# Semaphores set by four engines, routing without its own norm stage, and a last norm in half rows: a two-part transformer stack on one core

## The reference

```python
def layer_norm(x, g, b):
    xf = x.astype(jnp.float32)
    mu = jnp.mean(xf, -1, keepdims=True)
    var = jnp.mean(jnp.square(xf - mu), -1, keepdims=True)
    return ((xf - mu) * lax.rsqrt(var + LN_EPS) * g + b).astype(x.dtype)

def moe_swiglu(h2, w_router, w_gate, w_up, w_down):
    logits = (h2 @ w_router).astype(jnp.float32)
    top_logits, top_idx = lax.top_k(logits, TOP_K)
    top_w = jax.nn.softmax(top_logits, axis=-1)
...
    hid = jax.nn.silu(lax.ragged_dot(xs, w_gate, sizes)) * lax.ragged_dot(xs, w_up, sizes)
    y = lax.ragged_dot(hid, w_down, sizes)
...
        h = layer_norm((DN_ALPHA * h + mix).astype(h.dtype), ln_mix_g[layer], ln_mix_b[layer])
            ff = moe_swiglu(h.reshape(B * S, D), moe_router[j], moe_w_gate[j], moe_w_up[j], moe_w_down[j])
        h = layer_norm((DN_ALPHA * h + ff).astype(h.dtype), ln_ffn_g[layer], ln_ffn_b[layer])
```

## Time and profile before

| what | us |
|---|---|
| median of 3 runs (lowest, highest) | 3354.91 (3353.01, 3355.23) |
| the profiled execution, its own time | 3353.27 |
| its span, first to last instruction | 3351.4 |
| PE busy | 3111.8 |
| DVE busy | 2402.8 |
| ACT busy | 1788.5 |
| POOL busy | 189.6 |
| mean granted TensorE clock, share of full speed | 0.962 |

### The profile page before, as it was taken

The page is one execution under the profiler, slowest core; times in us unless marked ns, Lnnn a source line. Parts: engine busy times, 40 slices in busy tenths (PEclk is TensorE's granted clock), DMA queues, the critical chain, the costliest instruction groups (busy, mean ns, idle before and its releaser), DMA issues. The chain is left out here.

```text
span 3351.4 us, 46020 instructions
## 1 busy us (share of the span) xinstructions
PE 3111.8 (93%) x18426; PEld 2722.4 (81%) x18426; DVE 2402.8 (72%) x2698; ACT 1788.5 (53%) x2115; POOL 189.6 (6%) x101
## 2 busy tenths in 40 slices
PE   6998899998899899989998999996999999999997
PEld 5887688876688798988888998886888888888885
DVE  4664566898766666555766666655999999889997
ACT  3444444433244455544444454443777777777775
POOL 0000000002400001110000021100000000000000
PEclk9998899999999899999999999997999999999998
DMA  4552255443155433343554433433999999999995
GB/s 164 190 192 100 84 188 208 165 162 125 63 188 188 177 141 120 137 142 133 181 189 159 143 126 126 152 128 152 364 354 355 355 355 354 355 356 355 353 358 201
DMA packets 97415, 698.65 MB, mean 208 GB/s; under 512 B 10960, under 2 KB 11472, under 8 KB 13776
## 3 DMA queue, kind: packets, MB, share of 16 engines
q1 hardware_dynamic: 97232, 696.11, 56.2%
HBM read 693.97 MB, written 1.05 MB: 207 GB/s over the span
## 5 line engine op out<-in xcount | busy, mean ns | idle before, releaser
L890 PE MATMUL ps<-weight_high,act_parts 128*128 128x512 f32 (+2 forms) x2656 | 749.8, 364 | 13.7 <-DVE act_parts L2698 3.8
L890 PEld LDWEIGHTS ps<-weight_high,act_parts 128*128 128x128 f32 x2656 | 480.8, 191 | 93.1 <-issue 10.2
L890 PE MATMUL ps<-weight_low,act_parts 128*128 128x512 f32 (+2 forms) x1456 | 516.4, 355 | 0.0
L861 PE MATMUL ps<-act_parts,weight_high 128*128 128x512 f32 x1760 | 459.6, 395 | 9.4 <-DVE weight_low L716 8.6
L861 PEld LDWEIGHTS ps<-act_parts,weight_high 128*128 128x128 f32 x1760 | 319.1, 190 | 70.3 <-DVE weight_low L716 11.0
L890 PE MATMUL ps<-act_parts,weight_low 128*128 128x256 f32 x1312 | 374.5, 285 | 0.0
L669 ACT ACTIVATE weight_high<-ring 128x2048 fp32r<-128x2048 f32 x108 | 206.7, 1915 | 311.3 <-PE ps L861 232.8
L890 PE MATMUL ps<-act_parts,weight_high 128*128 128x256 f32 x1792 | 335.9, 289 | 6.9 <-DVE weight_low L2554 5.7
L716 DVE TENSOR_TENSOR weight_low<-ring,weight_high 128x2048 fp32r<-128x2048 f32 x108 | 247.3, 2291 | 126.7 <-ACT weight_high L669 126.7
L2554 DVE TENSOR_TENSOR weight_low<-ring,weight_high 128x2048 fp32r<-128x2048 f32 x82 | 190.2, 2320 | 199.3 <-PE ps L890 131.9
L890 PEld LDWEIGHTS ps<-weight_low,act_parts 128*128 128x128 f32 x1456 | 280.2, 192 | 35.8 <-issue 1.0
(11 more groups left out here) (444 smaller groups left out, 5811.4 us busy)
## 6 DMA issues: line engine op xcount, KB each, us to landing
ring<-in_l_moe_up SPq DMA_DIRECT2D x110, 1024.0 KB, 4.9
ring_more<-in_l_moe_down SPq DMA_DIRECT2D x110, 1024.0 KB, 4.9
ring<-in_l_w_in SPq DMA_DIRECT2D x92, 1024.0 KB, 4.8
vtm<-in_l_moe_gate SPq DMA_DIRECT2D x55, 1024.0 KB, 4.9
merged<-in_l_moe_gate SPq DMA_DIRECT2D x55, 1024.0 KB, 4.9
ring<-in_l_ffn_down SPq DMA_DIRECT2D x52, 1024.0 KB, 4.8
ring<-in_l_ffn_up SPq DMA_DIRECT2D x35, 1024.0 KB, 4.8
ring_more<-in_l_ffn_gate SPq DMA_DIRECT2D x32, 1024.0 KB, 4.7
```

Of the source, the lines that this page charges most:

```text
L861: return c.nc.tensor.matmul(c.ps[:, bank, :], still, c.act[:, k, :, :].rearrange("p s t -> p (s t)"), start=k == 0, stop=k == KD - 1, skip ...
L890: ins = nc.tensor.matmul(out, still[a], moving[b], start=first and n == 0, stop=last and n == 2, skip_group_check=True)
```

## The change

1. The block that set the semaphores is gone. `start_stage` issues its loads on SyncE without waiting for it, and the other four engines each set a quarter of the semaphores (39) at the beginning of that stage.
2. `norm_stage` is gone; `route_stage` takes its work. x is turned after scaling by the statistics alone. ScalarE applies gain and offset per column while it evicts each of eight pairs of 128x128 blocks, and TensorE makes the logits of a pair as soon as it is evicted. Beside that VectorE applies the gain and offset rows to x, and ScalarE makes the high part of x.
3. The comparisons of both row tiles are made in one instruction each. The products that count each list come before those that place the rows.
4. The low part of x, the softmax weights, and the high and low parts of weight units 0 and 1 move behind the branch, into `experts_stage`; for the skipped dense way a block `weights_stage` repeats the weights.
5. SyncE loads the rows of the last norm at the end of `route_stage`. The last norm works on half rows with two fused instructions each and stores each half.
6. Each engine loads `most` once and keeps it in its register for the later guarded blocks.

```diff
-def when(c):
+def when(c, name):
 
     def wrap(body):
         if c.condition is None:
             return body
 
         def guarded(eng):
-            with eng.If(c.condition(eng.value_load(c.most, min_val=0, max_val=T))):
+            if name not in c.most_loaded:
+                c.most_loaded[name] = eng.value_load(c.most, min_val=0, max_val=T)
+            with eng.If(c.condition(c.most_loaded[name])):
                 body(eng)
         return guarded
...
-def norm_stage(c, gain, offset, units):
...
+        @block.sync
+        def _(sp):
+            for n, row in enumerate(rows):
+                sp.dma_start(c.rowbuf[:, n, :], row.partition_broadcast(P)).then_inc(gains.sem, 16)
+            for u in range(MOE_UNITS_AHEAD):
+                units.load(sp, u)
+            sp.wait_ge(scaled.sem, scaled.base + 4)
+            for n, row in enumerate(last_rows):
+                sp.dma_start(c.rowbuf[:, n, :], row.partition_broadcast(P)).then_inc(gains.sem, 16)
 
...
         @block.vector
         def _(dve):
             link = lambda ins: c.vchain(dve, ins)
             V = nc.vector
+            for t in range(TT):
+                for h in range(2):
+                    link(V.bn_stats(small[:, 32 + 16 * t + 6 * h:38 + 16 * t + 6 * h], x[:, t, 512 * h:512 * h + 512]))
+                link(V.bn_aggr(small[:, 16 + 2 * t:18 + 2 * t], small[:, 32 + 16 * t:44 + 16 * t]))
+                V.tensor_scalar(small[:, t:t + 1], small[:, 17 + 2 * t:18 + 2 * t], LN_EPS, None, ALU.add)\
+                    .then_inc(summed.sem, 1)
+            for t in range(TT):
+                dve.wait_ge(rooted.sem, rooted.base + t + 1)
+                link(V.reciprocal(small[:, 6 + t:7 + t], small[:, 2 + t:3 + t]))
+                V.tensor_scalar(x[:, t, :], x[:, t, :], small[:, 16 + 2 * t:17 + 2 * t], small[:, 6 + t:7 + t],
+                                ALU.subtract, ALU.mult).then_inc(normed.sem, 1)
+            dve.wait_ge(gains.sem, gains.base + 32)
+            for t in range(TT):
+                dve.wait_ge(packed.sem, packed.base + (1, 5)[t])
+                V.tensor_tensor(x[:, t, :], x[:, t, :], c.rowbuf[:, 0, :], ALU.mult).then_inc(scaled.sem, 1)
+                dve.wait_ge(scaled.sem, scaled.base + 2 * t + 1)
+                V.tensor_tensor(x[:, t, :], x[:, t, :], c.rowbuf[:, 1, :], ALU.add).then_inc(scaled.sem, 1)
             dve.wait_ge(logits_made.sem, logits_made.base + 1)
+            link(V.tensor_copy(logits, ps[:, 0:TT, 0:E]))
+            other = logits.unsqueeze(2).to_broadcast([P, TT, E, E])
+            own = logits.unsqueeze(3).to_broadcast([P, TT, E, E])
+            V.tensor_tensor(choice.above, other, own, ALU.is_gt)
+            link(V.tensor_tensor(choice.equal, other, own, ALU.is_equal))
+            link(V.tensor_tensor(choice.equal, choice.equal, lower.unsqueeze(1).to_broadcast([P, TT, E, E]), ALU.mult))
+            link(V.tensor_tensor(choice.above, choice.above, choice.equal, ALU.add))
+            link(V.tensor_reduce(choice.rank, choice.above, axis=AX.X, op=ALU.add))
+            V.tensor_scalar(one, choice.rank, 0.0, None, ALU.is_equal)
+            link(V.tensor_scalar(two, choice.rank, 1.0, None, ALU.is_equal))
+            V.tensor_tensor(r.chosen, one, two, ALU.add).then_inc(chosen_made.sem, 1)
+            link(V.tensor_tensor(choice.tmp, one, two, ALU.subtract))
+            link(V.tensor_tensor(choice.tmp, choice.tmp, logits, ALU.mult))
+            link(V.tensor_reduce(s(0), choice.tmp, axis=AX.X, op=ALU.add))
             V.tensor_scalar(s(1), s(0), -1.0, None, ALU.mult).then_inc(diff_made.sem, 1)
             dve.wait_ge(placed.sem, placed.base + 1)
+            link(V.tensor_reduce(s(5)[:, 0:1], ps[:, 3, 0:E], axis=AX.X, op=ALU.max))
+            link(V.tensor_copy(r.most, s(5)[0:1, 0:1]))
+            dve.wait_ge(placed.sem, placed.base + 2)
             link(V.tensor_copy(r.place, ps[:, 2, 0:2 * E].rearrange("p (t e) -> p t e", t=TT)))
 
...
         @block.scalar
         def _(act):
+            for t in range(TT):
+                act.wait_ge(summed.sem, summed.base + t + 1)
+                nc.scalar.activation(small[:, 2 + t:3 + t], small[:, t:t + 1], ACT.Sqrt).then_inc(rooted.sem, 1)
+            for n in range(KD):
+                k = n // 2 + 4 * (n % 2)
+                act.wait_ge(packed.sem, packed.base + 2 + k % 4)
+                nc.scalar.activation(c.hT[:, k, :], norm_bank(c, k), ACT.Identity, scale=gain[:, k:k + 1],
+                                     bias=offset[:, k:k + 1]).then_inc(unloaded.sem, 1)
+            for t in range(TT):
+                act.wait_ge(scaled.sem, scaled.base + 2 * t + 2)
+                nc.scalar.activation(c.x_parts[0][:, t, :], x[:, t, :], ACT.Copy).then_inc(x_parts.sem, 1)
             act.wait_ge(diff_made.sem, diff_made.base + 1)
             nc.scalar.activation(s(2), s(1), ACT.Exp).then_inc(exp_made.sem, 1)
+
+        @block.tensor
+        def _(pe):
+            for t in range(TT):
+                pe.wait_ge(normed.sem, normed.base + t + 1)
+                for b in range(4):
+                    for k in (b, b + 4):
+                        last = nc.tensor.transpose(norm_bank(c, k)[:, P * t:P * t + P], x[:, t, P * k:P * k + P], c.ident)
+                    if t == 1 or b == 3:
+                        last.then_inc(packed.sem, 1)
+            for n in range(KD):
+                k = n // 2 + 4 * (n % 2)
+                pe.wait_ge(unloaded.sem, unloaded.base + n + 1)
+                for t in range(TT):
+                    last = nc.tensor.matmul(ps[:, t, 0:E], c.hT[:, k, P * t:P * t + P], router[:, k, :], start=(n == 0),
+                                            stop=(n == KD - 1))
+            last.then_inc(logits_made.sem, 1)
+            pe.wait_ge(chosen_made.sem, chosen_made.base + 1)
+            for t in range(TT):
+                last = nc.tensor.matmul(ps[:, 3, 0:E], c.ones, r.chosen[:, t], start=(t == 0), stop=(t == TT - 1))
+            last.then_inc(placed.sem, 1)
+            nc.tensor.matmul(ps[:, 2, 0:E], earlier, r.chosen[:, 0], start=True, stop=True)
+            nc.tensor.matmul(ps[:, 2, E:2 * E], earlier, r.chosen[:, 1], start=True, stop=False)
+            nc.tensor.matmul(ps[:, 2, E:2 * E], c.ones, r.chosen[:, 0], start=False, stop=True).then_inc(placed.sem, 1)
...
+def weigh_choice(c, dve, r, choice):
+
+    V, s = c.nc.vector, choice.column
+    link = lambda ins: c.vchain(dve, ins)
+    link(V.tensor_scalar(s(3), s(2), 1.0, None, ALU.add))
+    link(V.reciprocal(s(4), s(3)))
+    link(V.tensor_tensor(s(5), s(2), s(4), ALU.mult))
+    for t in range(TT):
+        link(V.tensor_scalar(choice.tmp[:, t], choice.two[:, t], s(5)[:, t:t + 1], None, ALU.mult))
+        link(V.scalar_tensor_tensor(out=r.weight[:, t], in0=choice.one[:, t], scalar=s(4)[:, t:t + 1], in1=choice.tmp[:, t],
+                                    op0=ALU.mult, op1=ALU.add))
+
+
+def weights_stage(c, r, choice):
+
+    with c.nc.Block() as block:
+        @block.vector
+        @when(c, "vector")
+        def _(dve):
+            weigh_choice(c, dve, r, choice)
 
 
...
                 pe.wait_ge(picked.sem, picked.base + e + 1)
+                if part:
+                    pe.wait_ge(x_parts.sem, x_parts.base + 3)
...
+            units.make_high(act, 0)
             for half in range(2):
                 take_gathered(0, half, half)
+            units.make_high(act, 1)
...
             pick(0)
+            dve.wait_ge(x_parts.sem, x_parts.base + 2)
+            nc.vector.tensor_tensor(c.x_parts[1], c.x, c.x_parts[0].bitcast(F32), ALU.subtract).then_inc(x_parts.sem, 1)
+            weigh_choice(c, dve, r, choice)
+            units.make_low(dve, 0)
             for half in range(2):
                 take_gathered(0, half, 2 + half)
+            units.make_low(dve, 1)
...
-    norm_stage(c, gain, offset, units)
-    route_stage(c, router, lower, earlier, r, units)
+    choice = Choice(c)
+    route_stage(c, rows, columns, last_rows, router, lower, earlier, r, units, choice)
     chain = c.vchain
     c.condition, c.vchain = lambda most: most <= SLOTS, c.gathered_chain
-    experts_stage(c, r, iota, units, ALPHA)
+    experts_stage(c, r, iota, units, ALPHA, choice)
     c.condition, c.vchain = lambda most: most > SLOTS, c.dense_chain
+    weights_stage(c, r, choice)
     spread_stage(c, r.weight, c.cat)
     ffn_stage(c, *weights, G, EXPERTS, c.cat, keep=ALPHA, add=1.0, ahead=units.loaded)
     c.condition, c.vchain = None, chain
...
+    sems = [s.sem for s in c.sig.values()]
...
         @block.scalar
         def _(act):
+            for sem in sems[0::4]:
+                nc.scalar.sem_inc(sem, START)
...
-            for n, row in enumerate(rows):
-                sp.dma_start(c.rowbuf[:, n, :], row.partition_broadcast(P)).then_inc(gains.sem, 16)
             for t in range(TT):
-                sp.wait_ge(added.sem, added.base + t + 1)
-                sp.dma_start(out[:, t, :], x[:, t, :]).then_inc(stored.sem, 16)
```

(21 more changed lines are left out.)

193 lines of the change are left out of this document (59 added, 134 removed).

## The result

The changed kernel took 3328.11 us (median of 4 runs, 3327.14 to 3328.75), the kernel before 3353.96 us (4 runs, 3351.13 to 3355.23): a ratio of 0.9921, 95% interval 0.9910 to 0.9933. The forecast was 3327.4. The profiled execution took 3328.18, with a span of 3326.1 for 3351.4, so 25.3 us are to be found in the trace. Several of the kernels here now and then have a run some 6 to 10 us longer (five of the 34 runs of the kernel before that stood beside the experiments lay at 3360 to 3365 us), and in the two profiles that caught one, those of the experiments with 26 full products and with `most` loaded each time, the loss lies in the first 1000 us or so, far from the change.

A forecast was written before the change was run, and what follows sets the result against it. TensorE, busy 93%, was taken as the bound, so only its idle places counted: 12.8 (start) + 10.2 (ahead of experts) + 3.7 (end) = 26.7 off 3353.27 gives 3326.6; half of 1.64 added, 3327.4. Range 3322.0 to 3334.0.

The forecast's parts named there:

- the cover: Start: 39 increments per engine, at most 3.3 us, hidden by the 5.78 us from x's load issue to first work.
- the start does not shrink: Start: the 13 us are something other than increments, so only 13.9 us stays of the gain, 3340.2 us; chance 5%.
- The template of the mixer's norm: Ahead of the experts: mixer's norm timings reused after the statistics, first transpose +4.6 us, first eviction +7.0, transposes end +8.3.
- The lower clock level: Routing logits: 32 instructions at a 0.20 us cadence on TensorE, taking 6.4 us and ending at +14.7.
- the rival of 32%: Routing: logits run at the higher clock level, paced by evictions, 3.2 us less, 3324.2 us; chance 32%.
- The cover behind the branch: Picks to first product: work moved onto VectorE takes 8.3 us, just under the 8.58 us there; thin by 0.3.
- The SyncE queue's seventh load: Experts' start: loads 7 and 8 go some 7 us after the branch, wanted most of a 17.9 us step later; nothing waits.
- the rival of a lasting lag of VectorE: Experts' loop: VectorE enters later and stays late, 0.6 us TensorE wait per step, 33 us, so 3360; chance 2%.
- 0.3 + 3 x (0.3 + b): End: skipped-stage boundaries, b between 0 and 1.24, taken 0.4: 2.4 us for 3.39, gain 1.0.
- three now, without a load: End: three skipped stages that no longer load the count, part of the 1.0 us gain there.
- The half-row operation: Last norm: four half-row operations of 0.69 us each (bounds 0.64 and 0.75), norm 5.9 us for 6.98, gain 1.0.
- A dear branch: End: skipped stages costing 1.5 us more than now; with thin covers, 3329 to 3334 us, chance 9%.

The follow-up runs named there:

- the last kernel: Changed kernel with 18 full products ahead of the routing transposes and the 156 increments shared by three engines, none on TensorE: 3324.75 us, run again 3324.23 us.

## Why the prediction was right

The gains were forecast at 26.7 us off the profiled execution, and the trace has 25.3: 0.54 less at the start, 0.10 less ahead of the experts, 0.27 less at the end and 0.60 lost between, against 0.11 in the loop. That the median came within 0.7 us of 3327.4 is in part luck: the forecast had 0.82 added for the distance between median and profiled execution, and the changed kernel shows no such distance (3328.11 and 3328.18).

**The start**, forecast 12.8, measured 12.26. The issue at 0.75 was right (0.74), and so was the cause. The step that was off by half a microsecond is the cover: the increments were priced at 84 ns on every engine and put at 3.3 us. They are 73 ns on ScalarE, 93 on VectorE and about 80 on GpSimd, but 154 on TensorE, whose 39 held the barrier past the landing of the loads; without them the first work came at 6.80, 6.80 and 6.62 in three profiles instead of 7.08. The rival "the start does not shrink" rested on no row showing an increment; the packed trace of the kernel before had all 156 of them, up to 13.20 us. The rule of the Trainium skill, "Advanced Engine Details and Errata", DMA Bandwidth Details, that an increment costs about a cycle, does not hold for increments as instructions in a queue: by it the start would not have shrunk.

**Between the start and the routing** the forecast had nothing and 0.60 went. It is no term of the change: none of the experiments touches this part, and those without an early loss took between 2268.9 and 2271.2 us over it.

**Ahead of the experts**, 10.2 against 10.10. The template of the mixer's norm gave the transposes (+4.6, measured +4.58) and the evictions (+7.0, +7.01). The lower clock level was the right choice against the rival of 32%: the logits ran at 1.2 GHz throughout. They began at +8.05 for +8.3 and took 6.83 us, not 6.4, and VectorE's copy behind them began at +14.92 for +14.7; its chain to the choice took 2.2 for 2.3, and the picks came at +21.28 for +21.2. The rival was sound in what it would pay: at the higher level, held there by full products, the first product came 3.1 to 3.7 us earlier in four profiles, and the forecast had put 3.2 on it. The cover behind the branch held to its thin margin: 8.58 us from picks to product, the same as before, with 0.46 us of room on VectorE. The SyncE queue's seventh load went out at 2304.82 and nothing waited for it.

**The loop** did as the forecast said: 1004.38 for 1004.49 us, and the rival of a lasting lag of VectorE did not come. The number is not that firm in itself: over all profiles this stretch takes either 1002.7 to 1002.8 or 1004.1 to 1004.7 us, and the two profiled runs of the last kernel have one each, 1002.7 and 1004.6 (from their first product, 2302.19 and 2301.77, to their statistics of the last norm, less the skipped stages).

**The end**, forecast 3.7, measured 3.43, by errors that nearly cancel. The early rows gave 1.56 for 1.5. The skipped stages gave 0.55 for 1.0: in the forecast's own form, 0.3 + 3 x (0.3 + b), 2.84 makes b 0.55 in place of 0.4. The step that failed there is "three now, without a load": GpSimd still makes its load in the last skipped block and comes to its barrier some 0.2 us after the other engines, and TensorE's branches take 0.22 and 0.37 us. The half-row operation took 0.75 and not 0.69, its upper bound, which made the norm 0.70 for 1.0. The last store's 256 KB ended 2.42 us after the last operation for 3.04 with 512 KB, 0.62 for the 0.2 that was taken. A dear branch was right to keep as a rival, but its bound of 1.5 us more than before was too small: the stages cost 5.45 to 5.87 us with 18 or more products added to TensorE's program, 2.1 to 2.5 above before, and the changed kernel escaped that by where its code lies, which the prediction didn't weigh.

## What to carry to other kernels

Look at what stands ahead of the first load: a loop over semaphores on one engine cost a little more (12.3 us) than the whole rework of the norm and router gave back (10.1), and it is undone by letting the loads go first and sharing the loop, with the smallest share for the engine that is slowest at it. Work moved behind a branch is free as long as the engine it lands on still shows a wait for another one at the end of that stretch, so read that wait (here 0.46 us) before moving more. And when an edit that shortens one stage shows no gain, read the waits of stages that it doesn't touch: code that is only skipped can become dear because other code moved it. A value that is loaded once per engine is free only if every engine meets it before the path that counts.

## What the runs showed of the hardware

An increment of a semaphore as an instruction of its own took 73 ns on ScalarE, 93 ns on VectorE, about 80 ns on GpSimd and 154 ns on TensorE, start to start in the packed traces; 156 of them on GpSimd held a barrier until 13.57 us.

TensorE's clock stayed at 2.4 GHz through the transposes and most of the logits behind 18 full products of 128 rows, and fell behind the same number of products of 32 rows of zeros. Whether rows, type or data make the difference was not tried.

Three skipped blocks took 2.84 us or 5.1 to 5.9; 26 tiny products on TensorE, a thousand us ahead of them, were enough to make the difference. In the views only VectorE's wait at the barrier shows it; the packed traces have it as one branch of TensorE, 0.37 to 0.47 us or 2.78 to 3.78, with a 16 KB packet on the instruction queue during the long ones. A load of the count into a register took 0.28 to 0.32 us in the skipped blocks on four engines and 0.49 us on GpSimd.
